# Parts of three attention stages moved into the projections ahead of them, in a one-core transformer kernel

## What is computed

```python
for i in range(2):                       # first block
    x = x + 0.5 * swiglu(rmsnorm(x), ...)
    proj = rmsnorm(x) @ w_in[i]          # 1024 -> 2560: q, k, v of 12 heads of 64, q of 4 memory heads
    mkv = rmsnorm(mem) @ w_mem_kv[i]     # 256 memory rows
    o_m = memory_attention(rms(q_m), rms(k_m), v_m)
    if i == 0:                           # "rel": chunked attention, bias by relative distance
        o_s = chunked_rel_attention(rms(q), rms(k), v, a_rel_bias)
    else:                                # "diff": 6 pairs of heads, rotary embedding
        a = softmax(s[0]) - lam * softmax(s[1])
        o_s = rmsnorm(a @ v, b_subln) * (1 - lambda_init)
    x = x + concat([o_s, o_m]) @ w_out[i]
    x = x + 0.5 * swiglu(rmsnorm(x), ...)
# second block: "moba", 8 heads of 128, bias by T5 bucket; one block of 256 keys, so plain causal attention
h = layer_norm(ALPHA * x + moba_attention(x, w_in, w_out, rel_bias))
y = layer_norm(ALPHA * h + moe_ffn(h))   # 32 experts, 4 for each token, all weights read once
```

## Time and profile before

| | |
|---|---|
| median of 3 runs | 2241.07 us (2240.88 to 2255.78) |
| profiled execution | 2244.66 us, span 2242.8 us |
| mean granted clock | 0.977 |
| TensorE, VectorE, ScalarE, POOL busy | 92%, 38%, 30%, 2% |
| DMA | 604 MB, 269 GB/s over the span |

### The profile page before, as it was taken

How to read it: one execution, slowest core, us unless ns; L and a number is a source line. 1 busy time by engine, 2 the same in 40 slices (tenths; PEclk the granted TensorE clock), 3 DMA queues, 4 the chain that set the end, 5 groups by cost and what they waited for, 6 DMA issues and landing times.

```text
span 2242.8 us, 27943 instructions
## 1 busy us (share of the span) xinstructions
PE 2064.1 (92%) x11973; PEld 1381.9 (62%) x11973; DVE 850.4 (38%) x993; ACT 679.8 (30%) x890; POOL 34.4 (2%) x26
## 2 busy tenths in 40 slices
PE   7999999999999997899998899998899889989886
PEld 6998777899899875799977644433333333333322
DVE  5555644555655575555543511111111111111112
ACT  5444454454554544444434201111011000110101
POOL 5000000000000000000000000000000000000000
PEclk9999999999999997899999999999999999999998
DMA  8555416555455541355544599999999999999995
GB/s 275 190 194 178 151 29 206 169 187 187 151 187 187 169 150 38 95 187 187 188 151 150 236 379 421 421 421 421 421 421 422 421 421 421 421 421 421 421 421 237
DMA packets 192471, 604.24 MB, mean 269 GB/s; under 512 B 12277, under 2 KB 105409, under 8 KB 143125
## 3 DMA queue, kind: packets, MB, share of 16 engines
q1 hardware_dynamic: 192372, 602.83, 70.8%
HBM read 601.70 MB, written 1.09 MB: 269 GB/s over the span
## 4 chain that ended last, share of the span: by engine, by line
PE 58%; DMA 31%; DVE 5%; ACT 2%; SPq 2%; issue 1%; DVEq 0%; ACTq 0%
DMA sb_w_free<-in_moe_w_gate_up 16%; PE ps L1360 14%; PE ps L1361 14%; PE ps L1362 14%; DMA sb_nat<-in_moe_w_gate_up 7%; DMA sb_raw<-in_moe_w_gate_up 7%; PE ps L1677 6%; PE ps L1686 2%; PE ps L1494 1%; PE ps L1533 1%; SPq L452 1%; PE ps L1503 1%; PE ps L1518 1%; DVE sb_w_lo L831 1%; DMA sb_raw<-in_ffn_w_up 1%
## 5 line engine op out<-in xcount | busy, mean ns | idle before, releaser
L831 DVE TENSOR_TENSOR sb_w_lo<-sb_raw,sb_w_hi 128x2048 fp32r<-128x2048 f32 x180 | 415.0, 2309 | 361.5 <-ACT sb_w_hi L578 361.1
L578 ACT ACTIVATE sb_w_hi<-sb_raw 128x2048 fp32r<-128x2048 f32 x180 | 343.9, 1914 | 296.5 <-PE ps L1362 284.1
L1360 PE MATMUL ps<-sb_xT_hi,sb_w_hi 128*128 128x256 f32 x1408 | 397.3, 282 | 6.5 <-DVE sb_xT_lo L852 6.5
L1362 PE MATMUL ps<-sb_xT_hi,sb_w_lo 128*128 128x256 f32 x1408 | 396.2, 281 | 0.0
L1361 PE MATMUL ps<-sb_xT_lo,sb_w_hi 128*128 128x256 f32 x1408 | 396.2, 281 | 0.0
L1360 PEld LDWEIGHTS ps<-sb_xT_hi,sb_w_hi 128*128 128x128 f32 x1408 | 265.9, 189 | 9.1 <-issue 4.5
L1361 PEld LDWEIGHTS ps<-sb_xT_lo,sb_w_hi 128*128 128x128 f32 x1408 | 266.0, 189 | 1.7
L1362 PEld LDWEIGHTS ps<-sb_xT_hi,sb_w_lo 128*128 128x128 f32 x1408 | 266.0, 189 | 0.0
L1677 PE MATMUL ps<-sb_raw,sb_xs 128*64 128x512 f32 x784 | 183.8, 599 | 17.6 <-DMA sb_raw<-in_moe_w_gate_up 17.3
L1677 PE MATMUL ps<-sb_w_free,sb_xs 128*64 128x512 f32 x744 | 174.2, 599 | 19.4 <-DMA sb_w_free<-in_moe_w_gate_up 19.2
L1360 PE MATMUL ps<-sb_w_hi,sb_xT_hi 128*128 128x512 f32 x384 | 153.3, 399 | 9.6 <-DVE sb_xT_lo L852 4.7
(11 more groups left out here) (237 smaller groups left out, 2269.0 us busy)
## 6 DMA issues: line engine op xcount, KB each, us to landing
sb_raw<-in_moe_w_gate_up SPq DMA_DIRECT2D x98, 1024.0 KB, 26.4
sb_w_free<-in_moe_w_gate_up SPq DMA_DIRECT2D x93, 1024.0 KB, 26.7
sb_w_free<-in_moe_w_down SPq DMA_DIRECT2D x51, 1024.0 KB, 26.7
sb_raw<-in_moe_w_down SPq DMA_DIRECT2D x46, 1024.0 KB, 26.3
sb_raw<-in_ffn_w_gate SPq DMA_DIRECT2D x44, 1024.0 KB, 5.3
sb_raw<-in_ffn_w_up SPq DMA_DIRECT2D x44, 1024.0 KB, 5.3
sb_raw<-in_ffn_w_down SPq DMA_DIRECT2D x44, 1024.0 KB, 4.9
sb_late_raw<-in_moe_w_gate_up SPq DMA_DIRECT2D x32, 1024.0 KB, 26.7
```

The source lines that it names most:

```text
L578: sc.activation(w_hi[:, c % CUT, :], raw[:, c % RAW, :], ACT.Copy).then_inc(hi_made, 1)
L831: ve.tensor_tensor(w_lo[:, c % CUT, :], raw[:, c % RAW, :], w_hi[:, c % CUT, :].bitcast(F32), ALU.subtract).then_inc(lo_made, 1)
L1360: pe.matmul(o, l_hi, r_hi, start=start, stop=False)
L1362: return pe.matmul(o, l_lo, r_hi, start=False, stop=stop)
```

## The change

- **Transposes and copies.** `turn_qk` becomes `turn_tiles(kind, tiles)`, called between chunks of the projection. In layers 0 and 1: tiles 12 to 15 behind chunk 4, scores(0) and scores(1) behind chunk 5, tiles 0 to 7 behind chunk 8; tiles 8 to 11 come behind values(0). ScalarE makes all 16 copies (`tile_copies`). In MoBA: tiles 0 to 7 behind chunk 4, 8 to 15 behind chunk 8, scores(0) and (1) behind chunk 9.
- **First maxima and exponentials** (`opening`) go into the projection: in layers 0 and 1 at n = 3, in MoBA at n = 5.
- **Squares.** For head norms 2 to 4 ScalarE squares the group from PSUM (Square) behind its copy. Scratch is `probT` or `more_raw`.
- **Loop order.** VectorE goes follow(n+1), lead(n+2), outputs(n). In the last round the transposes of output block 0 stand ahead of outputs. In layer 0 the groups' order becomes (block 0, heads 0 and 4), (block 1, heads 0 and 4), then heads 8 of both. In layer 1 the norm of the outputs is cut in two (`sub_norm`), block 0's ahead of follow(7).
- **Strips.** 8 strips go to `more_raw` and are stored and loaded ahead of chunk 4 of the projection; layer 0's last four go to `strip_b` behind it. The expert slot `more_raw` becomes slot 4 and waits for the last MoBA scores.

```diff
-        strip = sb("strip", [P, 12, REL_W], stack=early)
+        strip_b = sb("strip_b", [P, 4, REL_W], stack=early)
+        strip = more_raw[:].rearrange("p (h w) -> p h w", h=8)
...
 @block.sync
-                product_chunks(c_in(i), a["w_in"][i], IN_ORDER)
+                product_chunks(c_in(i), a["w_in"][i], IN_ORDER[:2])
+                if i == 0:
+                    store_rows(0, 12)
+                    load_strips(0, strip, 0, 8)
+                product_chunks(c_in(i) + 4, a["w_in"][i], IN_ORDER[2:])
                 product_chunks(c_out(i), a["w_out"][i], range(2))
                 if i == 0:
-                    load_strips(0, 12, c_out(0))
+                    sp.wait_ge(chunk_used, c_out(0))
+                    load_strips(0, strip_b, 8, 4)
...
-            for j in range(5):
-                if j:
-                    sp.wait_ge(lo_made, MOE_C0 - RAW + j)
+            for j in range(4):
+                sp.wait_ge(lo_made, MOE_C0 - RAW + j + 1)
                 expert_chunk("gate_up", 0, j, j)
+            sp.wait_ge(scored, u_moba + 4)
+            expert_chunk("gate_up", 0, 4, 4)
...
 @block.scalar
+                    if before_read:
+                        before_read(n)
...
+                    ins = sc.activation(dst[:, :, 512 * col:512 * (col + 1)], ps[:, bank:bank + 2, :], ACT.Copy)
+                    if heads_of is not None and 1 <= n <= 3:
+                        sq = head_squares(heads_of).rearrange("p (b w) -> p b w", b=TB)
+                        ins = sc.activation(sq, ps[:, bank:bank + 2, :], ACT.Square)
+                    ins.then_inc(proj_read, 1)
...
+                def between(n):
+                    if n == 2:
+                        tile_copies(i, kind, range(12, 16), 0)
+                    elif n == 3:
+                        opening()
+                    elif n == 4:
+                        tile_copies(i, kind, range(8), 2)
...
 @block.vector
-                for n in range(len(groups)):
-                    if n + 2 < len(groups):
-                        lead(n + 2)
-                    if n + 1 < len(groups):
-                        follow(n + 1)
-                    outputs(n)
+                def remainder():
+                    follow(0)
+                    for n in range(len(groups)):
+                        if n + 1 < len(groups):
+                            follow(n + 1)
+                        if n + 2 < len(groups):
+                            lead(n + 2)
+                        outputs(n)
+                        if groups[n]["diff"] and n >= 5 and n != 6:
+                            sub_norm(int(n == 7))
...
 @block.tensor
+                def between(n, h):
+                    if (n, h) == (2, 0):
+                        pe.wait_ge(heads_ready, 4 * i + 1)
+                        turn_tiles(kind, range(12, 16))
+                    elif (n, h) == (2, 1):
+                        pe.wait_ge(tiles_copied, 16 * i + 4)
+                        opening()
+                    elif (n, h) == (4, 0):
+                        pe.wait_ge(heads_ready, 4 * i + 3)
+                        pe.wait_ge(prob_made, u_layer(i) + 2)
+                        turn_tiles(kind, range(8))
...
+                def remainder(later_tiles=None, first_block=None):
+                    for n in range(len(groups)):
+                        if n == 0:
+                            pe.wait_ge(proj_read, last - 1)
+                        values(n)
+                        if n == 0:
+                            if later_tiles:
+                                later_tiles()
+                            pe.wait_ge(proj_read, last)
+                        if n and n + 2 < len(groups):
+                            scores(n + 2)
+                        if n == len(groups) - 1:
+                            pe.wait_ge(prob_made, u0 + len(groups))
+                            first_block()
+                        outputs(n)
+                        if n == 0:
+                            scores(2)
```

More of the change, by code:

```diff
@@ L206, in build @@
         m_u = bc
-        slots = ([more_raw[:]] + [raw[:, k, :] for k in range(4)] + [late_raw[:, k, :] for k in range(2)]
+        slots = ([raw[:, k, :] for k in range(4)] + [more_raw[:]] + [late_raw[:, k, :] for k in range(2)]
                  + [nat[:].rearrange("p b d -> p (b d)")] + [raw[:, k, :] for k in (4, 5)]
@@ L311, in attention_groups @@
                                dv=HD, v=("kvm", 256), o=SELF_W, n=4, diff=False) for b in range(TB)]
[L312 to L313 removed]
+            order = [(b, h0) for b in range(TB) for h0 in (0, 4, 8)]
+            if kind == "rel":
+                order = [(b, h0) for b in range(TB) for h0 in (0, 4)] + [(b, 8) for b in range(TB)]
+            if kind == "moba":
+                for b in range(TB):
                     for h0 in (0, 4):
@@ L337, in pr_view, with head_squares @@
             return pr[:, 0:TB * w].rearrange("p (b w) -> p b w", b=TB)
+        def head_squares(i):
+            return (probT[:].rearrange("p a b c -> p (a b c)"), more_raw[:, 0:1024])[i]
         def row_by_distance(heads):
@@ L1044, in outputs, with opening, remainder, sub_norm @@
                                          soft[:, p, 8:12].unsqueeze(2).to_broadcast([P, k, dv]), ALU.mult).then_inc(o_made, 1)
-                lead(0)
-                lead(1)
-                follow(0)
-                for n in range(len(groups)):
-                    if n + 2 < len(groups):
-                        lead(n + 2)
-                    if n + 1 < len(groups):
-                        follow(n + 1)
-                    outputs(n)
+                def opening():
+                    lead(0)
+                    lead(1)
+                def remainder():
+                    follow(0)
+                    for n in range(len(groups)):
+                        if n + 1 < len(groups):
+                            follow(n + 1)
+                        if n + 2 < len(groups):
+                            lead(n + 2)
+                        outputs(n)
+                        if groups[n]["diff"] and n >= 5 and n != 6:
+                            sub_norm(int(n == 7))
+                return opening, remainder
+            def sub_norm(b):
+                steps = (8, 13)[b]
+                ve.wait_ge(sub_step, steps)
+                ve.tensor_scalar(sums[:, b, 0:6], sums[:, b, 0:6], 1.0 / P, EPS, ALU.mult, ALU.add).then_inc(sub_ms, 1)
+                ve.wait_ge(sub_std, b + 1)
+                ve.reciprocal(sums[:, b, 0:6], sums[:, b, 0:6]).then_inc(sub_step, 1)
+                ve.wait_ge(sub_step, steps + 1)
+                for h in range(6):
+                    view = nat[:, b, h * P:(h + 1) * P]
+                    ins = ve.scalar_tensor_tensor(out=view, in0=view, scalar=sums[:, b, h:h + 1],
+                                                  in1=bc[:, 384:512], op0=ALU.mult, op1=ALU.mult)
+                ins.then_inc(sub_normed, 1)
             def layer_norm(n):
@@ L1370, in keep_busy, with turn @@
                         pe.matmul(ps[:, bank, 0:P], ident[:], ident[:], start=True, stop=True)
-            def turn(src, ready, count):
-                for b in range(TB):
+            def turn(src, ready, count, blocks=range(TB)):
+                for b in blocks:
                     pe.wait_ge(ready, count + b)
@@ L1502, in scores @@
                                 else:
-                                    ins = pe.matmul(at(h), flip[:], strip[:, h0 + h, m0:m0 + nk], start=False, stop=True)
+                                    row = strip[:, h0 + h, m0:m0 + nk] if h0 < 8 else strip_b[:, h, m0:m0 + nk]
+                                    ins = pe.matmul(at(h), flip[:], row, start=False, stop=True)
                     ins.then_inc(scored, 1)
```

304 lines of the change are left out of this document (165 added, 139 removed).

## The result

The changed kernel takes 2216.21 us (median of 4 runs, 2213.70 to 2217.56); the kernel before now has a median of 2247.48 (4 runs, 2240.88 to 2255.78), where the forecast started from 2241.07. The ratio is 0.986, 95% interval 0.981 to 0.990: 1.4% faster. The profiled execution has 2217.56 us and a span of 2215.7, against 2242.8 before: 27.1 us less, where 27.4 were forecast. Between the medians it is 31.3 us. What follows explains the 27.1 of the two profiles; the kernel before spreads over 15 us from run to run, the changed one over 4.

What follows compares the result with a forecast made beforehand. TensorE bounds up to about 1290 us, then the expert stream, which starts earlier as attention ends earlier. Savings of 4+16.5+6.9 = 27.4 us from the 2241.07 median give 2213.7, forecast 2214, range 2203 to 2229.

Steps and rivals of the forecast that it cites:

- The sum: Savings of the three stages added: layer 0 4, layer 1 16.5, MoBA 6.9, together 27.4 us.
- The frame: Expert weight stream ends last; an earlier end of the third attention starts it earlier one to one, 10 us to spare.
- The waits inside the projections at nothing: TensorE's new waits between projection chunks, for norms, cuts and copies, were costed at 0 us.
- The store: Row store ahead of the strips in SP's queue, layer 0 and MoBA: between nothing and 5.1 us, taken as 2.5.
- Layer 1's ring: Layer 1's attention loop: TensorE drops out of the ring; rounds go from 7.5 us to 5.5, 4.0 with one key block.
- the detour: Layer 1's loop end: follow(7) and the last mix queue behind the first half of sub_norm, 4.5 us.
- rival 4: Loop reorder fails: maxima wait behind mixes, rounds stay at 7 us, layer 1 loses 8 us of saving; 2222, chance 0.07.
- ScalarE as the bound: ScalarE bounds the projections' ends; layer 0 saves nothing, layer 1 11 us, MoBA 4; 2226, chance 0.18.
- 2265: Slower rival: short transposes and scores between chunks lower the clock, dense projection matmuls run at 1.2 GHz; 51 us, chance 0.05.
- 2204: Faster rival: clock holds through layer 1's and layer 0's ends and entries are shorter; 10 us more saved, chance 0.1.
- the table loads: Four extra ScalarE table loads, two per layer, 1.28 us each; rival with all on the path: 5.1 us, 2219, chance 0.03.
- The sign of being wrong: Wrong if projections grow by more than 5 and 7.3 us, or TensorE's idle time before probT's copies grows.

Runs made afterwards that it cites:

- the waits filled: Changed kernel with matmuls nobody reads in two TensorE waits at layer 1's end; layer 1 107.9 us against 109.7, span 2215.7 us.
- the delay: Changed kernel with MoBA's eight strips loaded three times ahead of chunk 4; MoBA's stage 110.8 us against 99.4, span 2221.3.

## Why the prediction was right

- **The sum.** 27.4 us were forecast, 27.1 measured in the profiled executions. By stage: 4 against 3.3, 16.5 against 16.8, 6.9 against 7.0. No stage was out by more than 0.7 us.
- **The frame.** That a saving ahead of the expert stream moves it one to one: MoBA's stage ended 27.6 us earlier, the span 27.1. For small savings this is loose: with the waits filled MoBA's stage ended 3.2 us earlier and the part behind took all of it back.
- **The waits inside the projections at nothing.** TensorE is full in all three. 5 us to spare in front of chunk 4 were forecast, 5.0 measured by the delay. The store, bounded by 0 and 5.1 us and put at 2.5, took 1.5 from its issue to the first strip's; the eight strips took 4.8 instead of 3.7, and the two errors cancel. On ScalarE's side nothing is to spare in layer 0: 2.99 us added made outputs(0) 3.0 later. I had put outputs(0) at 3.2 us behind the projection; it starts at 298.17, 2.7 behind.
- **Layer 1's ring.** Forecast rounds of 4.0, 3.9, 4.9, 5.5, 5.5; measured at L1081 4.4, 4.3, 4.9 and 5.3, and 5.3 to the end of the last exponentials at 871.9. Then the detour: 4.5 forecast, 4.0 measured, as the mixing starts at 875.88. Undoing the order cost 7.9 us, the 8 that rival 4 had. That rival falls.
- **MoBA.** The wait of 2.8 for probT behind the exponentials is 2.29, and the strips' wait is gone. The strips alone give 3.2; together with the stage's 7.0 this leaves 3.8 for the rest.
- **The other rivals.** ScalarE as the bound (2226) did not happen as a loss of the savings, though it stands at the edge in layer 0. The clock did not fall in the projections (1.00, 1.00, 0.98), nor did it hold in layer 1 (0.70): neither 2265 nor 2204. The "clocks near 1" behind the projections, which the prediction wanted to see, came in layer 0 and MoBA only. Of the table loads, those at 832.40 and 842.98 in layer 1 run while their user waits; the load at 825.50 is in the busy run, as counted. By the price in the Trainium skill, "ScalarE: Activation LUTs", section "What ACT_TABLE_LOAD costs", the median would have been 2224, 8 us above what was measured.
- **The sign of being wrong.** The prediction says that it is wrong if the projections grow by more than 5 and 7.3 us, or if TensorE's idle time before probT's copies grows. The projections stayed below that (4.7, 3.8 and 7.0, first to last matmul), but the idle time grew in all three stages, from 7.8 us to 11.9 together, and so the second sign spoke against a forecast that came true. It was ill chosen: with the order alone the wait grew in layer 1 from 1.4 to 5.4 us while the stage got shorter, and with the order undone it fell from 4.8 to 2.3. So it comes with the order: TensorE no longer waits for the mix and meets the next wait instead, that for the copy which ScalarE makes behind its exponentials.

What was right partly by luck: in layer 0 the same code varies by 2.8 us with the clock of its tail, nearly as wide as the saving, and the range of 2.3 to 6.0 was set for that reason. Layer 1 of the kernel before took 126.6 us in the profile that the sum starts from and 131.8 in another; from that one the same forecast would have been 5 us off. The agreement within 0.3 us is thus one of two profiles: between the medians the gain is 31.3 us, and 29.6 in the later rounds (2247.28 and 2217.68). The openings were undervalued in the runs behind the prediction: I expected 8 to 12 us for them alone, and undoing them cost 15.1. The pieces undone one at a time (7.9 for the order, 15.1 for the openings, and for the strips 3.2 in the kernel before) come to 26.2. They are no exact partition of the 27.1, since the order is worth 5.9 alone and 7.9 with the rest, each holds a share of the clock, and the turned tiles, layer 0's order of groups and the earlier transposes of output block 0 were not tried by themselves.

## What to carry to other kernels

Count the chain behind a moved matmul, not the matmul: 7.8 us of short scores put between dense chunks cost their own time there and freed 22.9 us behind: maxima and exponentials ran beside the projection, and part of TensorE's work behind it ran at the higher clock. In a loop whose stages hand over in a ring, look at which engine stands in it only by the order of its queue, and take it out; then look for what is queued ahead of the last step of the chain, here a norm with a root in it that held the mix for 4.0 us. Before work is put beside a full stage, find the slack of each engine in numbers; a delay put in for that measures it in one run.

## What the hardware showed beyond that

A wait of TensorE can cost more than its length. The 2.84 us in front of the tiles of layer 0 were followed by 10.8 us at a granted clock of 0.55, and the stage grew by 6.1, of which only 1.7 were idle time. Of the other profiles in which the rest of the change is in place, only that with the openings behind has a low clock near that place, and it has a wait of 2.58 us ahead of it; but in the kernel before a wait of 2.5 us in layer 0 was followed by none, so the length of the wait alone doesn't decide. The 7.9 us in MoBA's projection made the stage 11.4 longer. Matmuls without a reader in such a wait brought the clock back in one run: eight transposes went from 1.94 to 1.06 us behind fifteen of them. In layer 1, where VectorE and ScalarE are the chain, a higher clock helps little: at 0.77 instead of 0.70 TensorE was busy 2.5 us less and idle 1.7 more.

The same code can also have either clock from one execution to the next: layer 1's stretch of the kernel before was at 0.69 and, with only MoBA's strips moved, at 0.57, 5.2 us apart, though its waits came to 20.8 us in the slower profile and 22.1 in the other; what tips it was not found.
